# Norms of the second block: sums taken in the experts' additions, the weighting beside the squares, rows turned by a diagonal product

## The chip, the cores and the metric

One core of one Trainium2 chip runs one program. The metric is the time of one execution on the device in microseconds; the median of several runs counts. The engines named below: TensorE (PE, matrix products), VectorE (DVE), ScalarE (ACT), GpSimd (POOL) and SyncE (SP, which issues the transfers of weights).

## The reference, cut to what matters

Two transformer blocks in float32, one behind the other, over 256 tokens of width 1024. The first block ends with a mixture of 8 experts and a layer norm; the second has two layers, each beginning with an RMS norm, and ends with one more:

```python
# end of the first block
f = moe_swiglu(x, ...)                      # sum over 8 experts of gate * swiglu
x = layer_norm(ALPHA * x + f, ln_g[1, 1], ln_b[1, 1])

# second block
for l in range(2):
    h = rmsnorm(x, norm_g[l])               # x * rsqrt(mean(x*x) + 1e-6) * g
    proj = h @ w_in[l]                      # split into q, k, v, ga, iq, ik, iw, xr, gr, ma, mb
    ...                                     # sparse attention, recurrent unit, gates
    x = x + merged @ w_o[l]
return rmsnorm(x, final_g)
```

## The kernel before

**Tiles.** Tokens are two tiles t of 128 rows. `X[:, t, :]` holds the rows of tile t, with tokens on partitions; `XT` holds the same activations turned, with features on partitions, as a pair of a high and a low part. A product with weights in float32 is three matmuls of such parts (`mm3`, L854 to L856: high*high, high*low, low*high). Every weight piece of 128x1024 goes through SP (load into one of six raw buffers, L670), ACT (`hi`, cast of the high part, L1790) and DVE (`lo`, subtraction, L2416) before PE may use it; the event is `lo` of that piece. Five pieces fit at a time in the second block: a piece's buffer is freed by the use of an older piece, and the list `W.after[x]` says which pieces follow once x is used. `W.after["bar"]` are the first five pieces of layer 0: the four of `v0` and the first of `xr`.

**Order.** Each engine runs its own program in order; `up` raises an event, `at` waits for it. There is no planner: the order on each engine is that of the code.

**End of the experts.** `scatter(e, t)` on PE spreads expert e's result over the rows of tile t into banks 6 and 7; DVE adds the two halves to `N4.fa` (L3001; a copy, L2999 and above, for e = 0). After the last expert every engine reads `flag` and jumps over a second pass of the experts, which is needed only when an expert got more than 128 tokens; its body holds the same `silu` as the first pass.

**Norms.** Behind the jump DVE first makes the low parts of the five pieces (`after("bar")`), adds ALPHA*x (L3105), takes mean and variance by `bn_stats` (L2481 to L2489, root on ACT at L2280) and applies g and b in two more passes (L2497, L2499) to both tiles, tile after tile. For layer l ACT squares `X` with a running sum (L2290) and takes the root (L2292), DVE scales the rows into `L2.H` (L3120), PE turns them (`rows_to_cols`, transposes at L860, banks 6 and 7), DVE and ACT multiply by norm_g while the features are on partitions (L2468, L1850), then ACT casts the high part into `XT` (L1854) and DVE subtracts the low one (L2459). PE goes on with `rm_first`, the product of `v0` (first half of v): tile 0 over pieces 0 to 3, then tile 1, into banks 0 and 1; ACT copies them out at L2361. Then comes `xr`, in banks 0, 1, 2, 3 in turn, then `v1` (banks 2, 3), `ik`, `iw`, `iq` and the rest of the layer.

**Between the layers and at the end.** `out_proj` multiplies `merged` by w_o into banks 4 to 7: pieces 0 to 3 for both tiles, pieces 4 to 7 for tile 0 (event `half`), then for tile 1. DVE adds each half row to `X` (L3292). The last norm: ACT squares (L2403), root (L2405), DVE multiplies by the factor and by final_g (L3301), for which POOL loads a row (L841) after the last addition; tile 1's squares wait for tile 0's result. Then SP stores both tiles in one transfer (L695).

Of the kernel before, what the change touches and what calls it, by code (L numbers as in the profile page):

```python
# [10 lines left out]
ACT = mybir.ActivationFunctionType  # L11
# [43 lines left out]
    "act_deviation": ("o_sq", "o_sd", "ln_sq", "ln_sd", "h_ss", "h_sd", "scaled_a"),  # L55
# [7 lines left out]
    "dve_lo": ("lo_x", "lo_o", "lo_merge", "scaled"),  # L63
# [5 lines left out]
    "dve_norm": ("add", "ln_mean", "ln_p", "ln_diag", "ln_var", "ln_y", "rows", "h_ms", "h_rows", "resid", "final"),  # L69
# [196 lines left out]
def _program(nc, ctx, p, out):  # L266
# [32 lines left out]
    LNC = take(80)  # L299
# [117 lines left out]
    B2.tm = take(32)  # L417
# [9 lines left out]
    N4.sg = v3(take(2 * 512), 2)  # L427
    N4.hh = v3(take(2 * 512), 2)
# [6 lines left out]
    tm = take(32)  # L435
    N4.tmps = [tm[:, 0:16], tm[:, 16:32]]
# [36 lines left out]
    L2.H = L2.VV  # L473
# [3 lines left out]
    Stack.at = B2.base  # L477
    F_row, F_sq = take(D), take(D)
# [160 lines left out]

    TILES = [(0, 1), (0, 1), (1, 0)]  # L640
# [17 lines left out]
    def sync_program(sp):  # L658
# [32 lines left out]
        for c in range(moe_chunks, len(W.chunks)):  # L691
            load(W, MAIN, c)
        for t in range(2):
            sp.wait_ge(*at("final", t))
        sp.dma_start(out.rearrange("o (a p) d -> p (o a) d", p=128), X).then_inc(*up("stored", by=16))  # L695
        sp.wait_ge(*at("stored"))


    def pool_program(gp):
# [70 lines left out]
        for dst, src in ((z[:, 0:T].bitcast(I32), bcast(p["positions_2"][0], 128)), (cr, p["c_rope"]),  # L770
# [5 lines left out]
            gp.dma_start(dst, src).then_inc(*up("two_in", 0, by=16))  # L776
        for l in range(2):
# [61 lines left out]
        gp.wait_ge(*at("resid", 1, 1, 1))  # L839
        gp.wait_ge(*at("hi_merge", 1, 6))  # L840
        gp.dma_start(F_row, bcast(p["final_g_2"], 128)).then_inc(*up("final_g", by=16))  # L841


    def tensor_program(pe):
# [75 lines left out]
        def rm_first(mine, xt, b2, ready, ev):  # L920

            for t in range(2):
                for q, x in enumerate(mine):
# [10 lines left out]
                    if t:  # L934
                        k_.then_inc(*up("used", x))
                busy[b2[t]] = (*ev, t)
# [18 lines left out]
        def out_proj(ot, mine, banks4, ready):  # L955
# [18 lines left out]
            for k in range(4, 8):  # L974
                step(k, 1).then_inc(*up("used", mine[k]))
# [19 lines left out]
        tr(bank[5][:, 0:80], pr1[0:80, :])  # L995
# [649 lines left out]

        for l in range(2):
            t_ = T_l[l]
            for t in range(2):
                rows_to_cols(L2.H[:, t, :], ("h", l), t, at("h_rows", l, t))
# [73 lines left out]
            rm(t_["v1"], XT, (2, 3), ("v", l), c0=1)  # L1723
# [10 lines left out]
            fm(t_["iq"], XT, (0, 1, 2, 3), ("iq", l), pace=lambda nb: nb % 2)  # L1734
# [20 lines left out]
            out_proj(XT, t_["o"], (4, 5, 6, 7), o_ready)  # L1755
# [22 lines left out]
    def scalar_program(a):  # L1778
# [58 lines left out]
        def norm_cols(n, gcol, bcol):  # L1837

            for t in range(2):
                ts = slice(t * 128, (t + 1) * 128)  # L1840
                for g in range(2):
                    if g == 0:
                        a.wait_ge(*at("scaled", n, t))
                    else:
                        a.wait_ge(*at("cols", n, t, g))
                        for j in range(4):
                            k_ = 4 * g + j
                            o = bank[7][:, j * 128:(j + 1) * 128]
# [33 lines left out]
        for dst, src in ((pr1[0:32, :], p["ln_g"].rearrange("l i (a b) -> (l i a) b", b=128)),  # L1882
                         (pr1[32:64, :], p["ln_b"].rearrange("l i (a b) -> (l i a) b", b=128)),
                         (pr1[64:80, :], p["norm_g_2"].rearrange("l (a b) -> (l a) b", b=128)),
                         (pr2[0:64, :], p["a_conv_w"][0].rearrange("j (i c) -> (j i) c", c=128)),
                         (pr2[64:72, :], bi[0:1024].rearrange("(a b) -> a b", b=128)),
                         (pr2[72:73, 0:64], bi[1024:1088].unsqueeze(0)), (pr2[72:73, 64:128], bi[1024:1088].unsqueeze(0)),
                         (pr2[73:74, 0:64], bi[1088:1152].unsqueeze(0)), (pr2[73:74, 64:128], bi[1088:1152].unsqueeze(0))):
            a.dma_start(dst, src).then_inc(*up("par_in", 0, by=16))
# [373 lines left out]
        lane.finish(g)  # L2263
        a.wait_ge(*at("flag"))
# [12 lines left out]
        after("bar")  # L2277
        for t in range(2):
            a.wait_ge(*at("ln_var", 3, t))
            a.activation(N4.tmps[t][:, 15:16], N4.tmps[t][:, 14:15], ACT.Sqrt).then_inc(*up("ln_sd", 3, t))  # L2280


        for l in range(2):
            t_ = T_l[l]
            for t in range(2):
                tmp = B2.tm[:, 8 * t:8 * t + 8]
                a.wait_ge(*at("rows", 3, t) if l == 0 else at("resid", 0, t, 1))
                if l and t == 0:
                    a.wait_ge(*at("used", "c", T_l[0]["yb"][-1][0]))
                a.activation(L2.GA[:, 0:4, :].rearrange("p a b -> p (a b)"), X[:, t, :], ACT.Square, accum_out=tmp[:, 0:1]).then_inc(*up("h_ss", l, t))  # L2290
                a.wait_ge(*at("h_ms", l, t))
                a.activation(tmp[:, 2:3], tmp[:, 1:2], ACT.Sqrt).then_inc(*up("h_sd", l, t))  # L2292
            norm_cols(("h", l), LNC[:, 64 + 8 * l:72 + 8 * l], None)

            def to(dst, name, l=l):
                def f(i, m, nb, x):
                    a.wait_ge(*at("used", x))
                    a.copy(dst[:, i:i + m, :], pair(nb % 4, i, m)).then_inc(*up(name, l, i))  # L2298
                return f
# [65 lines left out]
            fm(t_["xr"], to(L2.GR, "xr"))  # L2365
# [7 lines left out]
            fm(t_["iq"], to(L2.IQ, "iq"), pace=lambda nb: nb % 2)  # L2373
# [20 lines left out]
            out_proj(t_["o"])  # L2394
        for t in range(2):
            tmp = B2.tm[:, 8 * t:8 * t + 8]
            a.wait_ge(*at("resid", 1, t, 1))
            if t:
                a.wait_ge(*at("final", 0))
            else:  # L2400
                a.wait_ge(*at("hi_merge", 1, 6))
                a.wait_ge(*at("resid", 1, 1, 1))
            a.activation(F_sq, X[:, t, :], ACT.Square, accum_out=tmp[:, 0:1]).then_inc(*up("h_ss", 2, t))  # L2403
            a.wait_ge(*at("h_ms", 2, t))
# [992 lines left out]
```

## Time and profile before

| | us |
|---|---|
| median of 3 runs | 2400.07 (2398.04 to 2403.33) |
| the profiled execution | 2402.19 |
| its span, first to last instruction | 2400.4 |
| PE busy | 2256.9 (94%) |
| DVE busy | 1703.9 (71%) |
| ACT busy | 1417.9 (59%) |
| POOL busy | 312.8 (13%) |
| mean granted TensorE clock | 0.971 |

A busy share says how long an engine had an instruction in work, not that the time hangs on it. What the time hangs on is seen in the chain that ended last, and in the waits and timelines around the places that the change touches: from the last expert to the first products of layer 0 (place A, some 1540 to 1590 us), from layer 0 to layer 1 (place B, 1967 to 2001) and the end (place C, from 2380).

### The profile page before, as it was taken

The page shows a single profiled execution, that of the slowest core. Times are in us where ns is not written, and L with a number is a line of the kernel's source. Part 1 is how long each engine was busy: PE and PEld are TensorE (multiplying, and loading weights), DVE is VectorE, ACT ScalarE, POOL GpSimd, SP SyncE. Part 2 cuts the span into 40 slices and gives each one's busy share as a digit, 9 for nine tenths or more (in the row PEclk, how much of TensorE's full clock was granted, in tenths as well). Part 3 has the DMA queues.
Part 4 walks back from the last instruction along what each step waited for, and adds up shares of the span by engine and source line. Part 5 has one row for each costly group of instructions (what it writes and reads, how often), then busy time and mean ns, then how long its engine had stood idle before and what let it go on. Part 6 is the DMA issues. An engine that isn't in the chain of part 4 may idle for free.

```text
span 2400.4 us, 34359 instructions
## 1 busy us (share of the span) xinstructions
PE 2256.9 (94%) x13872; PEld 1977.6 (82%) x13872; DVE 1703.9 (71%) x2175; ACT 1417.9 (59%) x1899; POOL 312.8 (13%) x312
## 2 busy tenths in 40 slices
PE   7889999989999999999999999689998989999897
PEld 7778999868878888888888888578888978888896
DVE  5634555888999999999999999744696244469623
ACT  5433444557777878787878787445557234564612
POOL 0510000000000000000000000026534003554300
PEclk9999999999999999999999999889999999999999
DMA  9421755428899999999999999646443465544342
GB/s 249 123 89 53 249 190 175 168 86 304 317 368 369 364 346 364 345 366 352 363 351 365 355 352 363 238 117 204 135 127 118 124 222 152 181 128 143 114 127 97
DMA packets 327933, 555.41 MB, mean 231 GB/s; under 512 B 23584, under 2 KB 164728, under 8 KB 327768
## 3 DMA queue, kind: packets, MB, share of 16 engines
q1 hardware_dynamic: 318128, 527.63, 63.2%
q0 software_dynamic: 8832, 24.93, 4.4%
q8 instruction: 113, 1.85, 0.3%
q10 hardware_dynamic: 808, 0.58, 0.1%
q14 instruction: 52, 0.43, 0.1%
HBM read 543.11 MB, written 9.96 MB: 230 GB/s over the span
## 4 chain that ended last, share of the span: by engine, by line
PE 81%; DVE 11%; ACT 4%; issue 3%; DMA 1%; SPq 0%; ACTq 0%; POOLq 0%; DVEq 0%
PE bank L854 22%; PE bank L856 22%; PE bank L855 22%; PE bank L895 5%; DVE parts L2416 3%; ACT parts L1790 2%; PE bank L860 2%; PE bank L1520 1%; PE bank L1675 1%; PE bank L1713 1%; PE bank L1006 1%; PE bank L1581 1%; DVE work L3130 1%; DVE work L3131 1%; DVE work L3183 0%
## 5 line engine op out<-in xcount | busy, mean ns | idle before, releaser
L2416 DVE TENSOR_TENSOR parts<-raw,parts 128x1024 fp32r<-128x1024 f32 x665 | 809.8, 1233 | 417.5 <-ACT parts L1790 393.6
L1790 ACT CAST parts<-raw 128x1024 fp32r<-128x1024 f32 x665 | 692.0, 1047 | 521.0 <-PE bank L856 506.2
L854 PE MATMUL bank<-cols,parts 128*128 128x256 f32 x1680 | 500.1, 298 | 16.9 <-DVE work L3239 5.5
L855 PE MATMUL bank<-cols,parts 128*128 128x256 f32 x1680 | 481.6, 287 | 1.9 <-issue 1.9
L856 PE MATMUL bank<-cols,parts 128*128 128x256 f32 x1680 | 481.1, 286 | 0.0
L2416 DVE TENSOR_TENSOR fast<-raw,fast 128x1024 fp32r<-128x1024 f32 x302 | 362.1, 1220 | 32.5 <-ACT fast L1790 14.7
L1790 ACT CAST fast<-raw 128x1024 fp32r<-128x1024 f32 x302 | 315.6, 1052 | 94.3 <-PE bank L856 87.5
L854 PEld LDWEIGHTS bank<-cols,parts 128*128 128x128 f32 x1680 | 329.3, 196 | 34.2 <-issue 17.5
L855 PEld LDWEIGHTS bank<-cols,parts 128*128 128x128 f32 x1680 | 329.1, 196 | 6.1 <-issue 5.4
L856 PEld LDWEIGHTS bank<-cols,parts 128*128 128x128 f32 x1680 | 328.6, 196 | 2.0 <-issue 2.0
L854 PE MATMUL bank<-parts,cols 128*128 128x512 f32 x740 | 293.1, 396 | 6.7 <-DVE cols L2890 3.5
L856 PE MATMUL bank<-parts,cols 128*128 128x512 f32 x740 | 289.4, 391 | 0.0
L855 PE MATMUL bank<-parts,cols 128*128 128x512 f32 x740 | 289.2, 391 | 0.0
L854 PEld LDWEIGHTS bank<-parts,cols 128*128 128x128 f32 x740 | 139.8, 189 | 36.8 <-issue 3.1
L856 PEld LDWEIGHTS bank<-parts,cols 128*128 128x128 f32 x740 | 139.6, 189 | 29.5
L855 PEld LDWEIGHTS bank<-parts,cols 128*128 128x128 f32 x740 | 139.9, 189 | 28.0
L786 POOL DMA_DIRECT2D scr_xr<-work x6 | 4.9, 818 | 1187.9 <-ACT work L2298 1187.9
L854 PE MATMUL bank<-fast,cols 128*128 128x512 f32 x380 | 149.0, 392 | 0.8 <-DVE fast L2416 0.8
L856 PE MATMUL bank<-fast,cols 128*128 128x512 f32 x380 | 148.0, 389 | 0.0
L855 PE MATMUL bank<-fast,cols 128*128 128x512 f32 x380 | 147.9, 389 | 0.0
L895 PE MATMUL bank<-work,raw 128*128 128x256 f32 x608 | 132.1, 378 | 0.0
L895 PEld LDWEIGHTS bank<-work,raw 128*128 128x128 f32 x608 | 114.8, 189 | 16.7
(380 smaller groups left out, 3275.2 us busy)
## 6 DMA issues: line engine op xcount, KB each, us to landing
raw<-in_moe_w_gate_dram SPq DMA_DIRECT2D x112, 1024.0 KB, 6.9
raw<-in_moe_w_up_dram SPq DMA_DIRECT2D x112, 1024.0 KB, 6.6
raw<-in_moe_w_down_dram SPq DMA_DIRECT2D x112, 1024.0 KB, 7.0
raw<-in_w_in_dram SPq DMA_DIRECT2D x76, 1024.0 KB, 5.6
raw<-in_a_w_in_dram SPq DMA_DIRECT2D x12, 1024.0 KB, 13.0
raw<-in_ffn_w_gate_dram SPq DMA_DIRECT2D x11, 1024.0 KB, 5.2
raw<-in_ffn_w_up_dram SPq DMA_DIRECT2D x11, 1024.0 KB, 5.1
raw<-in_ffn_w_down_dram SPq DMA_DIRECT2D x11, 1024.0 KB, 4.9
```

Of the source, the lines that this page charges most:

```text
L854: pe.matmul(o, l[0], r[0], start=start, stop=False)
L855: pe.matmul(o, l[0], r[1], start=False, stop=False)
L856: return pe.matmul(o, l[1], r[0], start=False, stop=stop)
L860: return pe.transpose(o, i, ident[0:n, 0:n])
L895: k_ = pe.matmul(bank[b][:, j * T:(j + 1) * T], w[:, k, q * 128:(q + 1) * 128], xt[:, k, :], start=k == 0, stop=k == kt - 1)
L1006: k = pe.matmul(o[rs, 64 * j:64 * j + 64], l[rs, j, :], r[rs, j, :], start=True, stop=True)
L1520: k = pe.matmul(bank[b][:, j * 128:(j + 1) * 128], X[:, t, kk * 128:(kk + 1) * 128], N4.P_[:, a, t, :], start=t == 0, stop=t == 1)
L1581: k = pe.matmul(bank[b][:, :], N4.PT[:, e % 2, t, :], N4.y[:, q, 512 * h:512 * h + 512], start=q == 0, stop=q == 1)
L1675: k = pe.matmul(bank[b][:, i * wd:(i + 1) * wd], L2.IQ[64 * par:64 * par + 64, h // 2, n * 128:n * 128 + 128], L2.IK[64 * par:64 * par + 6 ...
L1713: k = pe.matmul(bank[6 + q][0:88, j * T:(j + 1) * T], L2.WR[:, q, h + j, :], L2.XC[:, h + j, :], start=True, stop=True)
L1790: a.copy(dst[0], src).then_inc(*up(o + "hi", x))
L2416: v.tensor_tensor(dst[1], src, dst[0].bitcast(F32), ALU.subtract).then_inc(*up(o + "lo", x))
```

## The change

At the three places:

- The expert sums begin with ALPHA*x (expert 0), and the eighth expert's additions give the row sums with them. DVE's low parts of the weight pieces come between the steps of the norms (`h_lows`), and so do ACT's casts (`his`).
- The layer norm is mean, (fa - mean)*g on DVE beside squares with bias on ACT, root, then *1/sd + b; tile 0 is finished before tile 1.
- The RMS norms: DVE multiplies the rows by norm_g (`h_gains`; rows of norm_g and final_g are loaded by POOL into all partitions) beside ACT's squares (`h_deviation`). The factor 1/rms (`h_over`) goes on the diagonal of `LD[:, t, :]` (`h_diag`), and PE turns and scales the weighted rows by a product with it (`h_cols`, banks 2 and 3 for tile 0, 6 and 7 for tile 1). Tile 1's product stands inside `rm_first`, behind piece 2 of tile 0. For layer 1 tile 0's product stands inside `out_proj`, before the last piece of tile 1.
- The last norm works the same way; its last scaling is halved between DVE and ACT, and the output goes out in four stores.
- `xr` and `iq` begin in bank 2, `v1` uses banks 0 and 1. Empty roots (`root_table`) at three places. At the start three small loads, one transpose and one copy are left out.

```diff
@@ SP
-        sp.dma_start(out.rearrange("o (a p) d -> p (o a) d", p=128), X).then_inc(*up("stored", by=16))
+            for h, name in enumerate(("final", "final_a")):
+                cs = slice(512 * h, 512 * h + 512)
+                sp.wait_ge(*at(name, t))
+                sp.dma_start(rows_out[:, t, cs], X[:, t, cs]).then_inc(*up("stored", t, h, by=16))
@@ POOL
+        gp.wait_ge(*at("cos", 1))
+        gp.dma_start(HN.g[0], bcast(p["norm_g_2"][0], 128)).then_inc(*up("h_gain", 0, by=16))
...
+            gp.wait_ge(*at("hr_gated", l))
+            gp.dma_start(HN.g[l + 1], bcast(p["final_g_2"] if l else p["norm_g_2"][1], 128)).then_inc(*up("h_gain", l + 1, by=16))
@@ PE
+        def h_cols(l, t):
+            pe.wait_ge(*at("h_rows", l, t))
+            pe.wait_ge(*at("h_diag", l, t))
+            for g in range(2):
+                b = h_bank(t, g)
+                claim(b)
+                for j in range(4):
+                    cs = slice((4 * g + j) * 128, (4 * g + j + 1) * 128)
+                    k = pe.matmul(bank[b][:, j * 128:(j + 1) * 128], HN.G[l][:, t, cs], LD[:, t, :], start=True, stop=True)
+                k.then_inc(*up("cols", ("h", l), t, g))
...
-            rm_first(t_["v0"][0], XT, (0, 1), (("h", l),), ("v", l, 0))
+            rm_first(t_["v0"][0], XT, (0, 1), (("h", l),), ("v", l, 0), lambda l=l: h_cols(l, 1))
-            fm(t_["xr"], XT, (0, 1, 2, 3), ("xr", l))
+            fm(t_["xr"], XT, (2, 3, 0, 1), ("xr", l))
...
-            out_proj(XT, t_["o"], (4, 5, 6, 7), o_ready)
+            out_proj(XT, t_["o"], (4, 5, 6, 7), o_ready, (lambda: h_cols(1, 0)) if l == 0 else None)
@@ ACT
+        root_table(3)
         a.wait_ge(*at("flag"))
...
-        after("bar")
+        def h_deviation(l, t):
+            q = LT[:, 8 * t:8 * t + 8]
+            a.wait_ge(*at("rows", 3, t) if l == 0 else at("resid", l - 1, t, 1))
...
+            a.activation(HN.junk, X[:, t, :], ACT.Square, accum_out=q[:, 6:7]).then_inc(*up("h_ss", l, t))
+            a.wait_ge(*at("h_ss", l, t))
+            a.activation(q[:, 7:8], q[:, 6:7], ACT.Sqrt, bias=eps["h"], scale=1.0 / D).then_inc(*up("h_sd", l, t))
+        def h_norm(l):
...
+            his(0, 1)
+            if l == 0:
+                for t in range(2):
+                    q = LT[:, 8 * t:8 * t + 8]
+                    a.wait_ge(*at("ln_mean", 3, t))
+                    a.activation(HN.junk, N4.fa[:, t, :], ACT.Square, bias=q[:, 2:3], accum_out=q[:, 3:4]).then_inc(*up("ln_sq", 3, t))
+                    a.wait_ge(*at("ln_sq", 3, t))
+                    a.activation(q[:, 4:5], q[:, 3:4], ACT.Sqrt, bias=eps["ln"], scale=1.0 / D).then_inc(*up("ln_sd", 3, t))
+            for t in range(2):
+                h_deviation(l, t)
+                his(*((1, 3), (3, 5))[t])
+                for g in range(2):
+                    a.wait_ge(*at("cols", ("h", l), t, g))
+                    a.copy(XT[0][:, 4 * g:4 * g + 4, t * 128:(t + 1) * 128], v3(bank[h_bank(t, g)][:, :], 4)).then_inc(*up("hi_x", ("h", l), t, g))
...
+            if l == 0:
+                out_proj(t_["o"][:3])
+                root_table(4)
+                h_norm(1)
@@ DVE
+        def h_gains(l, t):
...
+            v.tensor_tensor(HN.G[l][:, t, :], X[:, t, :], HN.g[l], ALU.mult).then_inc(*up("h_rows", l, t))
+        def h_diag(l, t):
+            h_over(l, t)
+            v.tensor_scalar(LD[:, t, :], ident, LT[:, 8 * t + 6:8 * t + 7], None, ALU.mult).then_inc(*up("h_diag", l, t))
...
+        ln_gains(0)
+        ln_rows(0)
+        h_gains(0, 0)
+        ln_gains(1)
+        h_diag(0, 0)
+        ln_rows(1)
+        h_low(0, 0)
+        h_lows(0, 0, 2)
+        h_gains(0, 1)
+        h_diag(0, 1)
+        h_lows(0, 2, 3)
+        h_low(0, 1)
+        h_lows(0, 3, 5)
...
+            if l == 0:
+                h_lows(1, 0, 1)
             for t in range(2):
+                if t == 1 and l == 0:
+                    h_lows(1, 1, 2)
+                    h_low(1, 0)
                 v.wait_ge(*(at("used", t_["o"][7]) if t else at("half", t_["o"][7])))
                 for h in range(2):
                     ...
+                h_gains(l + 1, t)
+                if l == 0:
+                    h_diag(1, t)
+                else:
+                    h_over(2, t)
+                    v.tensor_scalar(X[:, t, 0:512], HN.G[2][:, t, 0:512], LT[:, 8 * t + 6:8 * t + 7], None, ALU.mult).then_inc(*up("final", t))
+            if l == 0:
+                h_lows(1, 2, 4)
+                h_low(1, 1)
+                h_lows(1, 4, 5)
```

## Rows read from the trace of the kernel before

**Rows 1.** The page's chain that ended last: shares of the span by engine.

```profile
PE 81%; DVE 11%; ACT 4%; issue 3%; DMA 1%; SPq 0%; ACTq 0%; POOLq 0%; DVEq 0%
```

**Rows 2.** Busy time by stretch; behind POOL: granted clock, DMA share, GB/s.

```profile
560.00:1540.00 980.00, 976.54 (x4543) 811.38 (x4541) 898.97 (x878) 765.13 (x823) 0.00 (x0) 1.00 0.97 355
1586.00:1590.00 4.00, 2.29 (x20) 2.25 (x19) 2.29 (x2) 2.02 (x3) 0.00 (x0) 1.00 1.01 361
1675.70:1677.00 1.30, 1.30 (x3) 0.67 (x3) 1.27 (x3) 0.00 (x0) 0.00 (x0) 0.51 0.53 109
1677.00:1681.00 4.00, 4.00 (x25) 3.59 (x24) 2.47 (x4) 0.00 (x0) 0.00 (x0) 0.73 0.83 262
```

**Rows 3.** Waits of PE, 1540 to 2401: total us, times, longest us.

```profile
PE bank L860 <- DVE work L3120: 31.2, 2, 24.0
...
PE bank L1655 <- DVE work L3130: 8.7, 4, 2.9
```

**Rows 4.** Timeline of DVE, place A: start us, us, line, operation, [idle before <-releaser].

```profile
1542.47 1.34 DVE L3001 TENSOR_TENSOR work<-work,bank 128x512 f32<-128x512 f32 x2 [0.24 <-PE bank L1581]
1546.79 5.77 DVE L2416 TENSOR_TENSOR parts<-raw,parts 128x1024 fp32r<-128x1024 f32 x5 [2.99 <-ACT parts L1790]
...
1570.14 0.69 DVE L2459 TENSOR_TENSOR cols<-bank,cols 128x512 fp32r<-128x512 f32 x1 [0.65 <-ACT cols L1854]
```

**Rows 5.** Timeline of ACT, place A.

```profile
1541.83 4.83 ACT L1790 CAST parts<-raw 128x1024 fp32r<-128x1024 f32 x5 [1.98 <-issue]
1546.68 1.28 ACT L2280 ACT_TABLE_LOAD   x1
...
1571.15 0.59 ACT L1854 CAST cols<-bank 128x512 fp32r<-128x512 f32 x1
```

**Rows 6.** Timeline of PE, place A.

```profile
1567.04 1.97 PE L860 MATMUL bank<-work 128*128 128x128 f32 x8 [23.95 <-DVE work L3120]
...
1587.78 0.36 PE L854 MATMUL bank<-cols,parts 128*128 128x256 f32 x1 [1.71 <-ACT work L2361]
```

**Rows 7.** Timeline of PE, place B.

```profile
1972.81 0.39 PE L856 MATMUL bank<-parts,cols 128*128 128x512 f32 x1
...
2001.03 0.36 PE L854 MATMUL bank<-cols,parts 128*128 128x256 f32 x1 [1.71 <-ACT work L2361]
```

**Rows 8.** The chain of waits in order of time: start us, us, what.

```profile
1972.75 0.23 PE bank L855
...
1987.51 0.43 PE bank L855
```

**Rows 9.** Timeline of ACT, place B.

```profile
1976.77 1.06 ACT L2290 ACTIVATE work<-work 128x1024 f32<-128x1024 f32 x1 [2.49 <-DVE work L3292]
...
1977.94 1.28 ACT L2292 ACT_TABLE_LOAD   x1
1979.23 0.20 ACT L2292 ACTIVATE work<-work 128x1 f32<-128x1 f32 x1
```

**Rows 10.** Timelines of DVE and SP, place C.

```profile
2385.72 1.28 DVE L3292 TENSOR_TENSOR work<-work,bank 128x512 f32<-128x512 f32 x2 [4.15 <-PE bank L856]
...
2391.43 1.28 DVE L3301 SCALAR_TENSOR_TENSOR work<-work 128x1024 f32<-128x1024 f32 x1 [1.46 <-DMA work<-in_final_g_dram]
...
2395.99 0.39 SPq L695 DMA_DIRECT2D out_dram<-work  x1
```

**Rows 11.** Lines L2510, L2522, L1297: ns min/median/max, first and last start us.

```profile
L2510 DVE SCALAR_TENSOR_TENSOR work<-work,bank x12: 680/684/689, 228.5 to 526.3; 128x512 f32<-128x512 f32 x12
...
L2522 DVE TENSOR_SCALAR work<-work x6: 286/288/290, 231.9 to 529.1; 128x128 f32<-128x128 f32 x6
...
L1297 PE MATMUL bank<-work x96: 275/275/275, 234.1 to 531.9; 128*128 128x128 f32 x96
```

**Rows 12.** DMA issues: count, KB each, median us from issue to landing.

```profile
raw<-in_w_in_dram SPq DMA_DIRECT2D x4, 256.0 KB, 3.5
out_dram<-work SPq DMA_DIRECT2D x1, 1024.0 KB, 4.0
```

More of the change, by code:

```diff
@@ L472, in _program @@
     L2.st = take(64)
-    L2.H = L2.VV
     L2.MA, L2.MB = L2.IQ, L2.KT
@@ L638, in _program @@
     late = {y for ys in LATE_LO for y in ys}
+    H_NEXT = [W.after["bar"], [y for x in T_l[0]["o"][3:] for y in W.after.get(x, ())]]
+    late.update(H_NEXT[1])
     TILES = [(0, 1), (0, 1), (1, 0)]
@@ L974, in out_proj @@
             for k in range(4, 8):
+                if k == 7 and between:
+                    between()
                 step(k, 1).then_inc(*up("used", mine[k]))
@@ L2283, in scalar_program @@
+        h_norm(0)
         for l in range(2):
             t_ = T_l[l]
[L2285 to L2292, printed above, removed]
@@ L2393, in scalar_program @@
             fm_raw(t_["yb"], merge)
-            out_proj(t_["o"])
-        for t in range(2):
[L2396 to L2404, printed above, removed]
-            a.activation(tmp[:, 2:3], tmp[:, 1:2], ACT.Sqrt).then_inc(*up("h_sd", 2, t))
+            if l == 0:
[3 more added lines that the diff above has]
+            else:
+                out_proj(t_["o"])
+                root_table(5)
+        for t in range(2):
+            h_deviation(2, t)
+            a.wait_ge(*at("f_over", t))
+            a.activation(X[:, t, 512:1024], HN.G[2][:, t, 512:1024], ACT.Copy, scale=LT[:, 8 * t + 6:8 * t + 7]).then_inc(*up("final_a", t))
     def vector_program(v):
@@ L2996, in scatter @@
                     if side and e == 0:
-                        v.tensor_copy(f, bank[6 + h][:, :]).then_inc(*up(o + "sum", e, t, h))
-                    else:
+                        v.scalar_tensor_tensor(f, X[:, t, 512 * h:512 * h + 512], ALPHA, bank[6 + h][:, :], ALU.mult, ALU.add).then_inc(*up(o + "sum", e, t, h))
+                    elif e < NE - 1:
                         if e:
@@ L3001, in scatter @@
                         v.tensor_tensor(f, f, bank[6 + h][:, :], ALU.add).then_inc(*up(o + "sum", e, t, h))
+                    else:
+                        v.wait_ge(*at(o + "sum", e - 1, t, h))
+                        v.scalar_tensor_tensor(f, f, 1.0, bank[6 + h][:, :], ALU.mult, ALU.add, accum_out=LT[:, 8 * t + h:8 * t + h + 1]).then_inc(*up(o + "sum", e, t, h))
             picks(0)
@@ L3100, in vector_program, with h_lows @@
             v.wait_ge(*at("o_y", NE - 1, 1))
-        after("bar")
-        for t in range(2):
-            if t == 0:
-                v.wait_ge(*at("sum", NE - 1, 1, 1))
-            v.scalar_tensor_tensor(X[:, t, :], X[:, t, :], ALPHA, N4.fa[:, t, :], ALU.mult, ALU.add).then_inc(*up("add", 3, t, 1))
-            norm_rows(3, t, N4.tmps[t], at("add", 3, t, 1))
-        scale_rows(3, N4.gb, lambda t: at("ln_y", 3, t))
+        def h_lows(l, i, j):
+            for y in H_NEXT[l][i:j]:
+                lo(W, MAIN, y)
@@ new lines, in h_gains, with h_over @@
+        def h_gains(l, t):
+            v.wait_ge(*at("rows", 3, t) if l == 0 else at("resid", l - 1, t, 1))
+            if t == 0:
+                v.wait_ge(*at("h_gain", l))
+            v.tensor_tensor(HN.G[l][:, t, :], X[:, t, :], HN.g[l], ALU.mult).then_inc(*up("h_rows", l, t))
+        def h_over(l, t):
+            q = LT[:, 8 * t:8 * t + 8]
+            v.wait_ge(*at("h_sd", l, t))
+            v.reciprocal(q[:, 6:7], q[:, 7:8]).then_inc(*up("f_over", t) if l == 2 else up("dve"))
+            v.wait_ge(*at("f_over", t) if l == 2 else at("dve"))
```

160 lines of the change are left out of this document (53 added, 107 removed).

## Prediction

> **What bounds the kernel now.** I read the chain of waits first [rows 1]: four fifths of the span are TensorE (PE), a tenth VectorE (DVE). So PE's work sets the length, and a change that leaves PE's work alone can only win where PE stands still. In the long expert stage it does not: busy 976.54 of 980 us at clock 1.00, with the DMA engines at 0.97 [rows 2]. After that stage 31.2 us go in two waits of PE for L3120, the scaled rows of the second block's norms, the longer 24.0 us [rows 3], and twice 1.7 us for L2361, the copy of v's first half out of its bank, right after `v0` [rows 6, 7]. The timelines show three places.
>
> Place A, from the last expert to layer 0's `xr`. DVE's last addition ends at 1543.81; after the branch on `flag` its next instruction starts at 1546.79, and that one is five low halves of weights (5.77 us) ahead of the norm [rows 4]. ScalarE (ACT) is past its branch at 1541.83 [rows 5]. PE stands 23.95 us until 1567.04, turns the rows, does `v0` (48 matmuls), and starts `xr` at 1587.78 after 1.71 us for the bank [rows 6]. Place B, layer 0 to 1: the last matmul of the output projection starts at 1972.81, `xr` of layer 1 at 2001.03 [rows 7]; on ACT a table load of 1.28 us stands between the squares and the root [rows 9]. Place C, the end: the last addition starts at 2385.72; the weighting waits for the DMA of `final_g` (1.46 us), tile 1's squares wait for tile 0's result, and the one store goes out at 2395.99 [rows 10].
>
> **The change, part by part.** I lay the new order out instruction by instruction from row durations: a three-operand pass over 128x1024 1.28 us [rows 10]; a two-operand one 1.2 (five in 5.77) and a low half of columns 0.69 [rows 4]; a high cast of weights 1.0 (five in 4.83), of columns 0.59 [rows 5]; squares 1.06 and some 0.2 for the sum [rows 9]; diagonal 0.29; a product of 128x128 with it 0.275 alone, and overlapped as they are, 8 in about 1 us at full clock [rows 11]; each [128,1] operation some 0.2, an estimate. A 512-column matmul takes 0.23 us of the chain at full clock, 0.43 at half [rows 8].
>
> *Sums in the additions.* The eighth expert's additions become a form with a running sum: 0.684 us as L2510 against 0.68, plus a readout of some 0.1 [rows 11]. The two of tile 1 are on the path: +0.2. Expert 0's four copies read X too; their bound is the same 0.68, in a stage that PE fills: 0.
>
> *Place A.* DVE leaves the branch at 1547.0 (by ACT's 1.98 us it would be 1546.0: bound -1). Mean 1547.2. Then DVE weights by g (to 1548.5) beside ACT's squares (to 1548.5). `root_table(3)` loads the root's table before the branch, but the skipped body uses another table, so I expect a load after it all the same: today's load at 1546.68 stands after it too [rows 5], hidden there; in the new order it falls between squares and root, as in [rows 9], +1.28. Root 1550.1, rows of tile 0 1551.6, weighted by norm_g 1552.85. ACT next waits for tile 1's mean (DVE: 1553.1), squares and roots it, and only then takes tile 0's h squares: root at 1556.0. Reciprocal and diagonal 1556.6, product 1557.6 and 1558.6; ACT casts two pieces first, columns high 1559.2, low on DVE 1559.9, then lows of pieces 0 and 1. PE starts `v0` at 1561.1, at half clock for about 4 us: pieces 0, 1, 2 end at 1567.1. Tile 1's product follows at 1568.1; but piece 3's low half is queued on DVE behind tile 1's column lows: high 1568.9, lows 1569.6, piece 3 1570.9. So PE waits about 2.8 us in the middle of `v0`. What such a gap costs is shown: after the 2.9 us wait for L3130 [rows 3] the clock reads 0.51 over 1.3 us and 0.73 over the next 4 [rows 2], i.e. half clock for 1.3 + 2.2 = 3.5 us, in which 1.65 us are lost. Piece 3 and tile 1 are 30 matmuls: 6.8 + 1.65, `v0` ends at 1579.4. `xr` starts in bank 2, so the 1.7 us wait is gone. 1587.8 - 1579.4 = **8.4 us**; with no second load and full clock 11.3; with half clock for all 30 matmuls behind the gap (0.2 more each, 6.0 in place of 1.65) 4.
>
> *Place B.* t=0 of the projection ends 24 matmuls, 5.4 us, before t=1, near 1967.8. DVE adds (1.3), weights (1.2); ACT squares from 1969.1, its table loaded after piece 2's casts, when ACT idles; diagonal at 1971.1. PE reaches the product at 1971.7, before the last 6 matmuls: no wait, ends 1974.0, against 1972.81 + 0.4. ACT casts two pieces, columns high 1973.7, low 1974.5. PE enters `v0` at 1974.0, does pieces 0 and 1 until 1976.7. Piece 2's low half is queued behind tile 1's additions, weighting, root and diagonal (1974.5 to 1977.8): 1979.0, a wait of 2.3 us. A gap of 1.7 leaves the clock at 1.00 (1586 to 1590 [rows 2]), one of 2.9 does not; 2.3 lies in the middle, and I take the dearer: -1.65. Then piece 2, product (1), piece 3, tile 1: 36 x 0.227 + 1 + 1.65 = 10.8, end 1989.8. 2001.0 - 1989.8 = **11.2 us**; 12.9 with the clock up; 5.5 if half clock holds for all 36 matmuls (7.2).
>
> *Place C.* Both tiles' additions stay where they are (last 2387.0). ACT squares at once, root 2388.5, reciprocal 2388.7; the weighting (1.28) runs beside it and the DMA for `final_g`, 4.0 us, is long done, issued after `hr_gated`. The last scaling is halved between DVE and ACT: no row has it; bound 0.2 (nothing but the fixed part) to 0.69 each, I take 0.6. The last quarter's issue is second on SP: 2389.4 + 0.4. The whole store took 4.0 us to land, a 256 KB load 3.5 [rows 12]; a quarter's floor is a quarter of 4.0, 1.0; I take 3.1 from the issue, nearer the row of its size. End 2392.9 against 2400.4: **7.5 us** (6.5 to 9.5).
>
> *The rest.* The 512 KB row of norm_g comes in during the expert stage: at 355 GB/s [rows 2] 1.4 us of DMA time, which PE sees only if it waits for weights, and it is idle for 3.5 us in all of the 980: 0 (bound -1.4). Layer 1's and the final row are issued by POOL after `hr_gated`; POOL has nothing else until the next `xr`. Three small loads, one transpose and one copy go from the start, where PE waits for the first weights: 0 (up to 0.5). Bank order of `xr`, `v1`, `iq` only rotates. SP's weight loads follow low halves; they are six buffers ahead: 0.
>
> The Trainium skill (ScalarE: Activation LUTs, What ACT_TABLE_LOAD costs) puts a switch at about 2.66 us, 1283 ns and a drain of 1380 ns. The trace agrees with the first figure; but not with a drain: from the load's start at 1977.94 to the root's at 1979.23 are 1.29 us [rows 9]. By the page, the load left in A would cost 1.4 us more and those taken out of B and C would give 1.4 more each: 28.5 in place of 27.1.
>
> Sum: 8.4 + 11.2 + 7.5 = **27.1 us**. The profiled execution took 2402.19 us (span 2400.4 and 1.8 around it), which gives 2375.1; the median of the three runs is 2400.07, 2.1 lower, so I forecast 2373.0.
>
> **Rivals.**
> R1, nothing is late inside `v0`: the branch costs 2 us, no second table load, full clock after the gaps. 11.3 + 1 + 12.9 + 9 = 34: 2366. For it: each step has its bound; against: the in-order DVE queue puts piece 3 (A) and piece 2 (B) behind other work whatever the rest does.
> R2, the hand-overs inside `v0` keep the clock at half for both `v0`: 4 + 5.5 + 7.5 = 17: 2383. For it: a matmul still takes 0.43 at 1987.51 [rows 8], in steady work; against: it rose 3.5 us after a 2.9 us gap.
> R3, slower: broken up by products and waits, `v0` leaves PE at half clock through `xr` too. `xr` is 11 x 24 matmuls of 256 columns, half of the 0.43 and 0.23 above, so 0.21 in place of 0.12 us each: 24 us a layer, 48 in both, on top of R2: 17 - 48, 31 slower, 2431. It decides once more than a third of both `xr` (17 of 48 us) runs at half clock. Against: [rows 2] show the clock back within 5.3 us.
> R4, what is moved costs PE as much in `v0` as it saved before: the change does nothing. It needs 27 us of waits in two stages that last 14 us each as laid out above, and leaves 2400.
>
> **How the numbers follow.** Forecast 0.58, R1 0.17, R2 0.20, R3 0.03, R4 0.02. 0.2% (4.8 us) is about what a measurement of this kernel can tell from no change. The first three are all faster by more: 0.95; same 0.02; slower 0.03. The range for 8 in 10: from R1's 2366 to R2's 2383.
>
> **What would show it.** A: DVE's first instruction after the branch is the mean, near 1547; a table load between ACT's squares and root; PE's `v0` from 1561, one gap of about 3 us in it; `xr` at 1579 and no wait for L2361. B: PE goes from projection to `v0` without a gap, with one of 2.3 us between pieces 1 and 2, clock half after it. C: four stores, the last some 7 us earlier than today's. The forecast is wrong if `xr` starts later than 36 us after the last expert addition (A), if PE waits for the first diagonal in B, or if slices after `v0` read a clock below 1.00 for over 6 us.

## The result and the profile after

The changed kernel takes 2375.42 us (median, 2372.75 to 2379.05) against 2400.74 (2398.04 to 2403.33): ratio 0.9896, 95% interval 0.9878 to 0.9913. The forecast was 2373.0, the range 2366 to 2383. The profiled execution took 2379.05 us, its span is 2377.2 against 2400.4, mean granted clock 0.976 against 0.971.

The page of the changed kernel: busy time of the engines, then the head of the chain of waits. PE's share rose because the same work stands in a shorter span.

```profile
PE 2261.4 (95%) x13903; PEld 1984.1 (83%) x13903; DVE 1695.3 (71%) x2152; ACT 1421.5 (60%) x1894; POOL 316.0 (13%) x314
PE 82%; DVE 12%; ACT 4%; issue 2%; DMA 0%; SPq 0%; ACTq 0%; DVEq 0%
```

The waits of PE (engine, line, what it waited for: us in total, times, longest): in place of 31.2 us for L3120 and 3.4 for L2361 [rows 3, 6] one wait of 13.2 us for the first diagonal, and waits for low halves at L2436: 2.53, 2.53 and 1.82 us in the places of the change, and one of 5.7 us at 16 us, where the kernel before waits 4.4 us too.

```profile
PE bank L1668 <- DVE work L3105: 13.2, 1, 13.2
PE bank L864 <- DVE parts L2436: 12.6, 4, 5.7
```

Place A on VectorE of the changed kernel (start us, us, engine line operation; in brackets the idle time before it and what ended it). These rows and the next answer to [rows 4, 5]: the first instruction behind the branch is now the mean of the sums (L3115).

```profile
1544.79 0.08 DVE L2985 DVE_READ_ACCUMULATOR work<-work,bank 128x1 f32 x1
1547.70 0.21 DVE L3115 TENSOR_SCALAR work<-work 128x1 f32<-128x1 f32 x1 [2.83 <-issue]
1550.83 0.16 DVE L3124 RECIPROCAL work<-work 128x1 f32<-128x1 f32 x1 [1.59 <-ACT work L2305]
1553.57 0.21 DVE L3115 TENSOR_SCALAR work<-work 128x1 f32<-128x1 f32 x1
1556.98 0.29 DVE L3105 TENSOR_SCALAR work<-work 128x128 f32<-128x128 f32 x1
1571.18 0.69 DVE L2479 TENSOR_TENSOR cols<-bank,cols 128x512 fp32r<-128x512 f32 x1 [3.78 <-ACT cols L2311]
1572.68 2.35 DVE L2436 TENSOR_TENSOR parts<-raw,parts 128x1024 fp32r<-128x1024 f32 x2
```

The same place on ScalarE: a table load (L2305) stands between squares and root.

```profile
1542.65 1.28 ACT L1816 ACT_TABLE_LOAD   x1 [0.24 <-issue]
1547.95 1.15 ACT L2303 ACTIVATE work<-work 128x1024 f32<-128x1024 f32 x1 [2.96 <-DVE work L3115]
1549.21 1.28 ACT L2305 ACT_TABLE_LOAD   x1
1550.51 0.29 ACT L2305 ACTIVATE work<-work 128x1 f32<-128x1 f32 x1
1556.45 0.29 ACT L2291 ACTIVATE work<-work 128x1 f32<-128x1 f32 x1
```

TensorE in the same kernel, places A and B (one of each kind of row); [rows 6, 7] answer to them. The products with the diagonal are L1668. Of the bracketed waits, the 2.53 us at 1563.65 stand before `v0`, and the 2.53 us at 1573.95 and the 1.82 us at 1973.47 are the two gaps in the middle of `v0` that the forecast speaks of. `xr` (1582.48 and 1985.19) follows without a wait: the copy of v's half holds nobody up.

```profile
1557.37 3.75 PE L1668 MATMUL bank<-work 128*128 128x128 f32 x16 [13.23 <-DVE work L3105]
1563.65 0.50 PE L864 MATMUL bank<-parts,cols 128*128 128x512 f32 x1 [2.53 <-DVE parts L2436]
1569.47 1.95 PE L1668 MATMUL bank<-work 128*128 128x128 f32 x16
1573.95 0.50 PE L864 MATMUL bank<-parts,cols 128*128 128x512 f32 x1 [2.53 <-DVE parts L2436]
1582.48 0.28 PE L864 MATMUL bank<-cols,parts 128*128 128x256 f32 x1
1965.59 1.95 PE L1668 MATMUL bank<-work 128*128 128x128 f32 x16
1973.47 0.50 PE L864 MATMUL bank<-parts,cols 128*128 128x512 f32 x1 [1.82 <-DVE parts L2436]
1975.77 2.75 PE L1668 MATMUL bank<-work 128*128 128x128 f32 x16
1985.19 0.28 PE L864 MATMUL bank<-cols,parts 128*128 128x256 f32 x1
```

The stretches of TensorE behind them (window, length, PE busy, granted clock, DMA share, GB/s): clock 0.50, the lower level of 1.2 GHz, through the first product; 0.95 to 1.00 before each of the two gaps in `v0`, half again after it, and back within 5 us.

```profile
1557.00:1561.00 4.00, 3.63 (x16) 0.50 0.00 0
1567.40:1571.40 4.00, 4.00 (x25) 0.95 0.49 174
1574.00:1578.00 4.00, 4.00 (x11) 0.58 0.48 134
1578.00:1582.00 4.00, 4.00 (x19) 0.99 0.01 4
1968.00:1972.00 4.00, 3.65 (x17) 1.00 0.79 256
1974.00:1978.00 4.00, 4.00 (x18) 0.57 0.50 134
```

Place C on VectorE [rows 10]: between the last additions and the scaling stand only ACT's squares and root and the reciprocal; the DMA for `final_g` holds nobody up.

```profile
2370.57 1.28 DVE L3321 TENSOR_TENSOR work<-work,bank 128x512 f32<-128x512 f32 x2 [1.92 <-PE bank L866]
2373.60 0.49 DVE L3327 TENSOR_SCALAR work<-work 128x512 f32<-128x512 f32 x1
```

The store queue of the same kernel: four stores of 256 KB, each landing in 2.2 us (median).

```profile
2368.68 6.24 SPq L704 DMA_DIRECT2D out_dram<-work  x4
```

**Where the time went.** I cut each span at the last expert addition, at the first matmul of `xr` of layer 0 and of layer 1. In each stretch I also summed, microsecond by microsecond, PE's busy time times (1 - granted clock): what half clock cost. The rest is the stretch's length at full clock, and it is the cleaner number. It has a limit: where PE at full clock runs ahead of VectorE, what the clock gives back turns into a wait and counts as length.

| us (at full clock + lost to half clock) | to last addition | A: to `xr` 0 | B: to `xr` 1 | C: to the end |
|---|---|---|---|---|
| before | 1525.3 + 18.5 | 40.3 + 3.6 | 400.6 + 12.6 | 391.0 + 8.4 |
| after | 1525.0 + 19.9 | 32.4 + 5.2 | 392.6 + 10.1 | 382.9 + 9.1 |
| difference | -0.3 + 1.4 | -7.9 + 1.6 | -8.0 - 2.5 | -8.1 + 0.7 |

As measured: +1.1, -6.36, -10.54, -7.32, together -23.2. Each place gave 8 us at full clock; the clock moved the rest about. In B, 0.8 of the 10.54 us lie in no place of the change, but some 240 us behind `xr`, where the kernel before loses 2.4 us to half clock and the changed one 1.7. Another 1.7 lie in the place itself: in layer 1's first products the kernel before loses 3.4 us to half clock and the changed one 1.7.

### The profile page after: what moved, and what is told of

It is laid out like the page before. It is cut to its first block, busy times and chain, and to the rows that moved or that the text cites. A ratio compares the mean times of both kernels' runs of the same rounds, so it can differ in the third digit from the quotient of the medians.

```text
span 2377.2 us, 34395 instructions
## 1 busy us (share of the span) xinstructions
PE 2261.4 (95%) x13903; PEld 1984.1 (83%) x13903; DVE 1695.3 (71%) x2152; ACT 1421.5 (60%) x1894; POOL 316.0 (13%) x314
## 4 chain that ended last, share of the span: by engine, by line
PE 82%; DVE 12%; ACT 4%; issue 2%; DMA 0%; SPq 0%; ACTq 0%; DVEq 0%
PE bank L864 22%; PE bank L866 22%; PE bank L865 22%; PE bank L905 6%; DVE parts L2436 3%; PE bank L870 1%; ACT parts L1816 1%; PE bank L1533 1%; PE bank L1701 1%; PE bank L1739 1%; DVE fast L2436 1%; PE bank L1019 1%; PE bank L1594 1%; DVE work L3154 1%; DVE work L3155 1%
## 5 line engine op out<-in xcount | busy, mean ns | idle before, releaser
L2436 DVE TENSOR_TENSOR parts<-raw,parts 128x1024 fp32r<-128x1024 f32 x665 | 809.2, 1231 | 400.7 <-ACT parts L1816 377.3
L2436 DVE TENSOR_TENSOR fast<-raw,fast 128x1024 fp32r<-128x1024 f32 x302 | 362.1, 1219 | 32.1 <-ACT fast L1816 14.9
```

The costliest lines, as they stand in the source:

```text
L2436: v.tensor_tensor(dst[1], src, dst[0].bitcast(F32), ALU.subtract).then_inc(*up(o + "lo", x))
```

## The experiments

All ran against the kernel before, whose median was 2396.33 us on the chip of e1 to e4, 2400.36 for e5 to e8 and 2399.64 for e9 to e11. A, B and C are the stretches of the table.

**e1: the low halves of the weights one piece earlier**, so that DVE doesn't reach the late one behind tile 1's column lows.

```diff
-        h_lows(0, 2, 3)
+        h_lows(0, 2, 4)
         h_low(0, 1)
-        h_lows(0, 3, 5)
+        h_lows(0, 4, 5)
@@ layer 1
-                    h_lows(1, 1, 2)
+                    h_lows(1, 1, 3)
-                h_lows(1, 2, 4)
+                h_lows(1, 3, 4)
```

> The changed kernel with DVE's low half of piece 3 (layer 0) put before tile 1's column lows, and that of piece 2 (layer 1) before tile 0's column lows and tile 1's additions. Theory (the queue order on DVE makes the gaps inside v0, and each gap also costs the clock afterwards): the gap of 2.53 us before piece 3 in layer 0 and that of 1.81 us before piece 2 in layer 1 go, with the half clock behind them: 4.5 us less in place A, 3.0 to 3.4 less in place B, 7.5 in all, about 2368. Rival 1 (the half clock behind the gaps comes from the narrow products, not from the gaps): only the gaps go, 2.5 + 1.8 = 4.3 less. Rival 2 (tile 1's diagonal becomes late instead in B): B gains under 1.

2362.8 us (2362.01 to 2363.58), ratio 0.9858 [0.9838, 0.9878]. A 29.7 + 3.6, B 390.7 + 6.6: the waits fell by 2.7 and 1.9, the length of the two gaps, and in this profile each fall of the clock behind them went too (1.6 and 1.7 us). It is 33.5 us under the kernel before, the changed kernel 25.3 us on its own chip: 8.2 more, 7.5 expected; e9 and e10 compare the two on one chip. TensorE in e1, all of place A: one gap is left.

```profile
1555.05 3.75 PE L1668 MATMUL bank<-work 128*128 128x128 f32 x16 [13.19 <-DVE work L3105]
1561.34 0.50 PE L864 MATMUL bank<-parts,cols 128*128 128x512 f32 x1 [2.53 <-DVE parts L2436]
1567.19 1.95 PE L1668 MATMUL bank<-work 128*128 128x128 f32 x16
1568.89 0.47 PE L864 MATMUL bank<-parts,cols 128*128 128x512 f32 x1
```

**e2: the root's table loaded behind the branch.**

```diff
         lane.finish(g)
-        root_table(3)
         a.wait_ge(*at("flag"))
...
             his(0, 1)
             if l == 0:
+                root_table(3)
```

> The changed kernel with the empty root of place A behind the branch on flag, after the first cast, where ACT stands 2.96 us until the mean. Theory (the second load between squares and root, 1.28 us, is on the path): 1.3 us less in place A, and only one load of the root's table there. Rival 1 (tile 1's mean decides when ACT goes on, so the load is hidden): 0. Rival 2 (a switch costs 2.66 us as the skill's page on ScalarE has it): 2.7 less.

2370.66 us (2369.09 to 2371.83), 0.989 [0.987, 0.9911]. ScalarE in e2: one load where there were three (for the empty root, for the cast behind the skipped body, for the first root), and it lies in the wait for the mean.

```profile
1539.77 1.05 ACT L1816 CAST parts<-raw 128x1024 fp32r<-128x1024 f32 x1 [1.91 <-issue]
1540.84 1.28 ACT L1865 ACT_TABLE_LOAD   x1
1545.21 1.15 ACT L2303 ACTIVATE work<-work 128x1024 f32<-128x1024 f32 x1 [2.88 <-DVE work L3115]
```

The wait for the first diagonal is 12.25 in place of 13.23 us. It is not the whole 1.28, since VectorE left the branch 0.3 us later (3.13 in place of 2.83 behind its last instruction). A is 31.3 + 6.4: 1.1 won in waits, 1.2 given back by the clock, so that A as measured (37.68) is what it was. Rival 2's 2.7 us are out: from the load's start to the root's are 1.30 us in the changed kernel, and taking the load away gave 0.98.

**e3: the banks of `xr`, `v1`, `iq` as before.**

```diff
-            fm(t_["xr"], XT, (2, 3, 0, 1), ("xr", l))
+            fm(t_["xr"], XT, (0, 1, 2, 3), ("xr", l))
-            rm(t_["v1"], XT, (0, 1), ("v", l), c0=1)
+            rm(t_["v1"], XT, (2, 3), ("v", l), c0=1)
```

> The changed kernel with the banks of xr, v1 and iq as before (xr from bank 0). Theory: PE waits for the copy of v's first half again, 1.7 us in each layer, 3.4 in all, clock unharmed. Rival 1: the copy comes in time since ACT has cast its pieces earlier now: 0. Rival 2: a gap of 1.7 us costs the clock too now: 3.4 + 2 x 1.6 = 6.6 more.

2376.4 us (2373.8 to 2378.99), 0.9911 [0.9889, 0.9934]. The wait is back in both layers, and A and B grow by 1.8 and 2.1 us at full clock; the clock stays at 1.00 behind it in A. PE before `xr` of layer 1:

```profile
1987.50 0.35 PE L864 MATMUL bank<-cols,parts 128*128 128x256 f32 x1 [1.71 <-ACT work L2382]
```

**e4: rows scaled on VectorE and turned by a transpose**, in place of the product with a diagonal.

```diff
-            v.tensor_scalar(LD[:, t, :], ident, LT[:, 8 * t + 6:8 * t + 7], None, ALU.mult)...
+            v.tensor_scalar(HN.G[l][:, t, :], HN.G[l][:, t, :], LT[:, 8 * t + 6:8 * t + 7], None, ALU.mult)...
-                    k = pe.matmul(..., HN.G[l][:, t, cs], LD[:, t, :], start=True, stop=True)
+                    k = tr(..., HN.G[l][:, t, cs])
```

> The changed kernel with the weighted rows scaled in place on DVE (0.75 us after the root, for 0.29 of the diagonal) and turned by transposes, as before, in place of products with the diagonal. Theory (a product with the diagonal is two matmuls of 128 columns on PE, 16 for a tile, 3.75 us at half and 1.95 at full clock, a transpose one): 8 transposes take 1.97 and 1.0; place A 1.8 - 0.5 less for tile 0 and 0.9 less for tile 1, 2.2 together; place B 0.3 to 1.3 less; 2.5 to 3.5 in all. Rival 1 (the product's pairs only count double in the records): nothing on PE, DVE's 0.5 more twice: 1 us more. Rival 2 (transposes don't bring the clock up): half clock lasts longer in v0, 1 to 2 more.

2371.17 us (2368.43 to 2372.55), 0.9895 [0.9875, 0.9916]. A 31.4 + 3.7, B 391.7 + 6.0: 1.0 and 0.9 less at full clock; with the 0.9 that the first turn loses less to half clock 2.8, where 2.5 to 3.5 stood. In whole times it cannot be seen: 25.2 us under the kernel before, the changed kernel 25.3. The scaling costs VectorE 0.76 in place of 0.29 us and the turn half: eight matmuls in 1.94 us at half clock and 1.04 at full, against sixteen in 3.75 and 1.95.

```profile
1554.96 1.94 PE L870 MATMUL bank<-work 128*128 128x128 f32 x8 [13.88 <-DVE work L3106]
1566.15 1.04 PE L870 MATMUL bank<-work 128*128 128x128 f32 x8
1569.88 0.50 PE L864 MATMUL bank<-parts,cols 128*128 128x512 f32 x1 [2.69 <-DVE parts L2436]
```

Behind that gap of 2.69 us the clock did not fall: the next 512-column matmuls take 0.40 us each. So the length of a gap alone does not tell whether the clock falls, and e5 and e9 say the same.

**e5: one store.**

```diff
-            for h, name in enumerate(("final", "final_a")):
-                cs = slice(512 * h, 512 * h + 512)
+            for name in ("final", "final_a"):
                 sp.wait_ge(*at(name, t))
-                sp.dma_start(rows_out[:, t, cs], X[:, t, cs])...
+        sp.dma_start(rows_out, X)...
```

> Edit: one store of both token tiles after all four quarters of the result are there, in place of four stores. Theory (the quarters save what the last landing is shorter): in the changed kernel the last quarter's store goes out about 2.2 us before the end, and in the kernel before one store of 1024 KB took 4.0 us to land, so the stretch from the last layer's first multiplication of the second block (xr1) to the end grows by 1.8 us, from 392.0 to about 393.8 less what the clock does between; the time about 2377. Rival (the end is set by something else, the semaphore and the queue's own closing): no change in that stretch.

2375.13 us (2371.41 to 2376.37), 0.9893 [0.9869, 0.9917]. C 384.6 + 8.2 against 382.9 + 9.1: the quarters are worth 1.7 us, as the shorter landing says. In whole times it cannot be seen. Place A, which e5 does not touch, is of use too: it is 33.7 + 1.9 where the changed kernel has 32.4 + 5.2. The granted clock reads 1.00 behind both waits of 2.53 us, and PE then ran ahead of VectorE and waited 0.79 us between them. TensorE in e5, and its stretch behind the second of these gaps:

```profile
1571.50 0.50 PE L863 MATMUL bank<-parts,cols 128*128 128x512 f32 x1 [2.53 <-DVE parts L2435]
1571.50:1575.50 4.00, 4.00 (x18) 1.00 0.52 132
```

**e6: layer 1's first product behind the output projection.**

```diff
-            out_proj(XT, t_["o"], (4, 5, 6, 7), o_ready, (lambda: h_cols(1, 0)) if l == 0 else None)
+            out_proj(XT, t_["o"], (4, 5, 6, 7), o_ready)
...
-            if l == 0:
-                h_cols(0, 0)
+            h_cols(l, 0)
```

> Edit: in layer 1 the product of token tile 0 is issued after the output projection and not inside it. Theory (the last matmuls of the output projection hide the chain from the columns' eviction to their low part, 2.53 us in place A): a gap of about 2.5 us opens before v0, the gap of 1.82 us before piece 2 shrinks or goes because VectorE has caught up, so xr0 to xr1 grows by 0.7 to 2.5 us, and by 1.7 more if TensorE's clock falls after the gap: 403.4 to 406.9 against 402.7. Rival (TensorE waits for the weights' low parts there whatever the products' place): the gaps only move, xr0 to xr1 stays within 0.5 us of 402.7.

2374.05 us (2370.27 to 2375.55), 0.9888 [0.9864, 0.9912]. A miss for the most part. B is 394.2 + 5.0: 1.6 us more at full clock, within the 0.7 to 2.5, but the clock lost 5 us less in this profile, so that B as measured (399.17) fell. And the gaps are not where I put them: 0.56 us before `v0`, and the later one grew from 1.82 to 2.19. The late piece stayed late.

**e7 and e8: a better order.** Both have e1 and e2, the two means first on VectorE, and the diagonal of tile 0 before tile 1's first norm; e8 has e4's transposes too.

```diff
-        ln_gains(0)
-        ln_rows(0)
-        h_gains(0, 0)
-        ln_gains(1)
-        h_diag(0, 0)
-        ln_rows(1)
-        h_low(0, 0)
-        h_lows(0, 0, 2)
+        ln_mean(0)
+        ln_mean(1)
+        ln_gains(0)
+        ln_rows(0)
+        h_gains(0, 0)
+        h_diag(0, 0)
+        ln_gains(1)
+        ln_rows(1)
+        h_lows(0, 0, 1)
+        h_low(0, 0)
+        h_lows(0, 1, 2)
```

> Edit: the low parts of the weights' pieces early (as in e1), the root's table loaded behind the branch (as in e2), the means of both token tiles first on VectorE, the diagonal of tile 0 before tile 1's first norm, and the first piece's low part before the columns' low part. Theory (the branch is left at the same time, and behind it the order of VectorE and ScalarE sets when the first product starts): the wait before the first product falls from 13.2 us by 1.0 (table) and about 3 (tile 1's work out of the way) to about 9.3; v0 without a later gap; last addition to xr0 28.5 to 30 us against 33.2 in e1; time 2357 to 2360. Rival (what comes late then is the low part of tile 1's columns or a weight piece, and a gap of 2 to 3 us opens in v0 with a fall of the clock behind it): 33 us, 2361 to 2363, no faster than e1.

> Edit: as e7, and the row's factor is multiplied into the rows (0.65 to 1.3 us of VectorE a tile) and the tile is turned by transposes, one recorded matmul per 128x128 block where the product with a diagonal has two. Theory (each product costs TensorE twice a transpose): the turning of a tile costs about 1 us at full clock and 2 at half in place of 1.95 and 3.75, of which the longer VectorE operation gives back up to 1.0 in tile 0: last addition to xr0 1 to 2 us under e7, xr0 to xr1 about 1 us under e1's 397.3; time 2355 to 2358. Rival (the longer scaling on VectorE makes the low parts late): equal to e7 or 1 us slower.

e7: 2360.5 us (2355.76 to 2363.03), 0.9832 [0.9806, 0.9858], A 25.4 + 2.0, B 390.6 + 8.4. e8: 2357.19 us (2352.58 to 2358.57), 0.9825 [0.9802, 0.9847], A 24.8 + 2.6, B 390.3 + 5.8. The first wait fell to 9.06 us, and A (27.4) beat its expectation; the whole time of e7 lies 0.5 us above the expected 2357 to 2360, that of e8 inside 2355 to 2358. The transposes gave 0.6 and 0.3 us, less than the 1 to 2 expected: in e8 the lows are what `v0` waits for (2.45 us). TensorE in e7, from the first product: no gap over 1.01 us, and in the stretches below no fall of the clock.

```profile
1552.68 3.76 PE L1668 MATMUL bank<-work 128*128 128x128 f32 x16 [9.06 <-DVE work L3105]
1557.07 0.48 PE L864 MATMUL bank<-parts,cols 128*128 128x512 f32 x1 [0.63 <-DVE parts L2436]
1561.63 0.50 PE L864 MATMUL bank<-parts,cols 128*128 128x512 f32 x1 [1.01 <-DVE parts L2436]
```

The stretches of TensorE in e7, columns as above:

```profile
1552.60:1556.40 3.80, 3.72 (x16) 0.50 0.00 0
1560.00:1564.00 4.00, 2.99 (x17) 1.00 0.90 266
1564.00:1568.00 4.00, 4.00 (x24) 1.00 0.48 130
```

**e9, e10, e11: the changed kernel, e1 and e8 again, on one chip.**

> The changed kernel itself, on the same chip as the two versions beside it. Theory (what differs from profile to profile outside the places of the change is the clock, in pieces of about 1.7 us): with the time that TensorE worked at half clock taken out, the stretches come to within 0.5 us of 32.4 (last addition to xr0), 392.6 (xr0 to xr1) and 382.9 us (xr1 to the end), while as they stand they differ by up to 5; ratio to the kernel before 0.989 to 0.992. Rival (the stretches differ by waits, not by the clock): the corrected lengths differ by more than 1 us as well.

> The version with the weights' low parts one piece earlier, on the same chip as the changed kernel. Theory: 4.6 to 5 us fewer than the changed kernel at full clock (2.7 in the first place, 1.9 in the second) and up to 3.3 of clock, so 4.5 to 8 us below it, and not 12 as across the two chips' medians. Rival (the gain stands as in the earlier pair of runs): 12 us below it.

> The version with the low parts early, the table behind the branch, the new order of the norms and transposes, on the same chip. Theory: at full clock 7.6 (first place) + 2.3 (second) = 9.9 us under the changed kernel and 5.2 under the version with the low parts alone, with the clock's pieces beside it: 10 to 18 under the changed kernel, 4 to 8 under the other. Rival (its order saves nothing that is seen outside one profile): within 2 us of the version with the low parts alone.

| | time us | ratio | A | B | C | lost in all |
|---|---|---|---|---|---|---|
| e9 | 2376.75 | 0.99 [0.9882, 0.9918] | 32.4 + 6.1 | 392.6 + 9.2 | 382.9 + 7.8 | 46.6 |
| e10 | 2363.05 | 0.9848 [0.9828, 0.9869] | 29.7 + 4.4 | 390.5 + 7.8 | 383.3 + 3.3 | 36.6 |
| e11 | 2357.25 | 0.9831 [0.981, 0.9852] | 24.3 + 2.8 | 390.0 + 7.7 | 383.3 + 4.2 | 33.5 |

A, B and C at full clock come back to 0.1 us in e9, and to 0.5 in the others (the stretch before them, which no experiment touches, only to 2.6: 1522.7 to 1525.3 over all profiles; and A of e5, as said, is 1.2 longer). e11 is the best version: 19.5 us under the changed kernel on the same chip, medians against medians, 10 to 18 expected. But my theory for e10 fell: it is 13.7 us under e9, not 4.5 to 8. The waits give 4.4 (2.7 + 2.1 less 0.4 in C). The rest is clock as far as the profiles show it, and most of it lies away from the gaps: behind the last addition e10 loses 15.5 us to half clock against 23.1 in e9 (e1 15.3 against 24.4 in the first profile). Of the 8 to 9 us between them only 1.7 (e10) and 3.3 (e1) stand behind the gaps, and 4 to 5 are in C, where nothing differs but when it starts. And e9, which is the changed kernel itself, does not fall behind the gap of 1.82 us in B:

```profile
1976.51 0.50 PE L864 MATMUL bank<-parts,cols 128*128 128x512 f32 x1 [1.82 <-DVE parts L2436]
1976.50:1980.50 4.00, 4.00 (x26) 1.00 0.44 115
```

## Why the prediction came out

**Right, and shown.** The three places, and within each the order of what ends last. DVE's in-order queue puts piece 3 in A and piece 2 in B behind tile 1's work: the gaps are 2.53 and 1.82 us (2.8 and 2.3 said), and e1 removes both. The table load between squares and root came in spite of the empty root before the branch; e2 shows it is the branch that undoes it. The bank order is worth 1.8 and 2.1 us a layer (1.7; e3). C: 7.5 said, 7.32 measured, and e5 shows the quarters' share. The place itself, from the last addition to the end, fell from 13.4 to 5.4 us, 8.0 in all; 0.7 more half clock elsewhere in the stretch hid the surplus. The sums cost 0.69 us and a readout of 0.08 each, as said, but the two of tile 1 take 1.34 us together, as the plain additions did: the +0.2 was nothing. R4 and R3 are out: the granted clock is 1.00 through the first 24 us of `xr` in A and in B, and no stage gave its gain back. R1 fails on the gaps; R2 on the clock, which came back within 5 us of each.

**Luck: the clock behind the gaps.** I took the length of a gap as what decides whether the clock falls, and the dearer case for the one in B. In the profile the clock fell behind both, as said. But the same gap of 1.82 us cost nothing in e9, and the same 2.53 us cost nothing in e5: the reading by length is not borne out, and the 1.65 us in B were right by chance.

**The step that failed: the product with the diagonal.** I wrote "a product of 128x128 with it 0.275 alone, and overlapped as they are, 8 in about 1 us at full clock". A tile takes 16 recorded matmuls, not 8: two for each 128x128 block, 1.95 us at full clock and 3.75 at half, where 1.0 and 2.0 stood in the sum. [Rows 11] gave one matmul's length, and I did not ask how many of them one call makes, though the rows had it: 6 diagonals (L2522) beside 96 product matmuls (L1297) are 16 for each diagonal. From the last addition, A comes to:

| us | said | measured |
|---|---|---|
| to the first product | 12.6 | 12.5 |
| first product to `v0` | 4.5 | 6.3 |
| pieces 0 to 2 | 6.0 | 5.8 |
| second product | 1.0 | 1.95 |
| gap | 2.8 | 2.5 |
| piece 3 and tile 1, half clock included | 8.5 | 8.5 |

Together 35.4 against 37.6. My own bound was 36 us for this stretch, so by it the forecast of A was wrong: 6.36 us won where 8.4 stood. e4 confirms the cause from the other side: with one matmul a block the same turn takes 1.94 and 1.04 us, and A is 1.0 us shorter at full clock and 1.5 in clock.

**The same step in B, partly hidden.** B: 11.2 said, 10.54 measured, of which 0.8 came from half clock in a stretch that the change does not touch. The place itself gave about 9.8, 1.4 less than said: two products take 1.95 us each at full clock where 1 stood, 1.9 more (the second shows 2.75, but 0.8 of that is the half clock behind the gap, which the sum has on its own), and the gap was 0.5 shorter. The total held (2375.4 for 2373.0) because the failed term is small beside the three gains: it took 2.7 us from A and 1.9 from B, of which shorter gaps and the end of the kernel gave some 1.3 back.

Two slips of the working change nothing: R4's "two stages that last 14 us each" last 18.3 and 15.8 us as laid out, and half clock for all 36 matmuls in B leaves some 5.6 us, not 5.5.

## What to carry to other kernels

Lay the new order out on each in-order queue and look for what stands behind the newly moved steps: the piece that PE needs next must not be queued behind work that waits for another engine; a low half made one piece earlier (e1) was worth 4.6 us of waits, more than the change of banks in both layers (3.9). Count the recorded matmuls of a call, not the calls, and give work behind a long wait the lower clock. When small edits are compared, take half-clock time out of each stretch first: lengths at full clock repeated to 0.5 us (but for A of e5, 1.2) where whole times of the same kernel spread over 8. Do not price a gap by its length alone: the same gap cost 0 or 1.7 us of clock here.

## What the runs showed of the hardware

- Half clock costs come in pieces. Within a layer the loss falls at the same four places (about 50, 88, 178 and 240 us behind `xr`), each time 0, about 1.4 to 1.7, or 2.4 to 3.4 us. The kernel before at the last of them (2.4 us):

```profile
1826.00:1830.00 4.00, 2.10 (x7) 0.50 0.77 267
1830.00:1834.00 4.00, 4.00 (x24) 0.66 0.00 0
```

And the changed kernel there (1.7 us):

```profile
1824.00:1828.00 4.00, 4.00 (x23) 0.59 0.01 2
1828.00:1832.00 4.00, 4.00 (x37) 1.00 0.00 0
```

- The clock fell behind gaps of 1.82 us (B of the changed kernel, e3 and e5), 2.32 us (e4, B) and 2.53 us (A of the changed kernel, e2, e3, e6 and e9), and stayed up behind 1.71 us (e3, before `xr`), 1.82 us (B of e2 and e9), 2.19 us (e6, B), 2.53 us (e5, A) and 2.69 us (e4, A). So one and the same gap goes either way. What decides is open; the start time of the gap differs in all of these. The Trainium skill (TensorE: Matmul & The Clock Gate, The HAM clock gate) says that the moment of the change depends on where a kernel's work falls in a cycle that runs on by itself; the traces agree in so far as the same gap of 1.82 us cost 0 (e9) or 1.7 us (the changed kernel). Why e1 and e10 lose 8 us less than the changed kernel in places that are alike was not settled.
- At the jump on `flag`, a loaded value, VectorE stands 2.8 to 3.1 us between its last instruction and the first behind it, in the kernel before as in every version of the changed one.
- The empty root before the branch made a table load (1.28 us at 1540.92), and ScalarE's first cast behind the branch made another; without it (e2) the cast needed none, and squares and casts ran in the root's table.
